# S5 split by token group, each half woven beside the other group's SwiGLU, two side steps for each main step

## The reference, cut to what matters

```python
x <- LN0(alpha*x + 0.5*SwiGLU_1(x))
x <- LN1(alpha*x + Mix_l(x))
x <- LN2(alpha*x + 0.5*SwiGLU_2(x))

def step(s, uc):                       # S5, 64 groups of 16 channels, 64 complex states per group
    bu = jnp.einsum('bcgh,gph->bcgp', uc.astype(jnp.complex64), b_bar)
    a_cum, s_loc = lax.associative_scan(_s5_combine, (a_elems, bu), axis=1)
    s_all = s_loc + a_cum * s[:, None]
    y = jnp.real(jnp.einsum('bcgp,ghp->bcgh', s_all, cm))
    return s_all[:, -1], y
...
g = jax.nn.gelu(y.astype(x.dtype))
return (g @ w_out) * jax.nn.sigmoid(g @ w_gate), s_re, s_im
```

## Time and profile before

| | us |
|---|---|
| device time, median of 3 runs | 2738.49 (2734.43 to 2738.73) |
| device time of the profiled execution | 2735.0 |
| span of its core in the profile | 2733.3 |
| mean granted TensorE clock | 0.939 of full speed |
| PE busy | 2436.1 (89%) |
| PEld busy | 2287.8 (84%) |
| DVE busy | 1707.0 (62%) |
| ACT busy | 998.7 (37%) |
| POOL busy | 496.3 (18%) |
| read from HBM | 370.35 MB, 138 GB/s over the span |

### The profile page before, as it was taken

How to read it: one execution, slowest core, us unless ns; L and a number is a source line. 1 busy time by engine, 2 the same in 40 slices (tenths; PEclk the granted TensorE clock), 3 DMA queues, 4 the chain that set the end, 5 groups by cost and what they waited for, 6 DMA issues and landing times. The chain is left out here.

```text
span 2733.3 us, 43046 instructions
## 1 busy us (share of the span) xinstructions
PE 2436.1 (89%) x17245; PEld 2287.8 (84%) x17245; DVE 1707.0 (62%) x2660; ACT 998.7 (37%) x1486; POOL 496.3 (18%) x559
## 2 busy tenths in 40 slices
PE   7999999989989999999999989994408799999996
PEld 7999989988876677988999989993306798999995
DVE  6666665666644556767555676555894467667554
ACT  3434443334432334424333344332203344434332
POOL 0711100033000122012100132005910022103003
PEclk9999999999999999989999999997557899999997
DMA  7665554344466865445555545541003555665452
GB/s 182 180 176 159 176 171 129 113 120 135 125 186 212 253 182 136 141 111 149 167 147 151 149 138 157 147 131 20 1 4 47 124 148 153 181 178 159 146 151 77
DMA packets 658616, 383.55 MB, mean 140 GB/s; under 512 B 29842, under 2 KB 629778, under 8 KB 658418
## 3 DMA queue, kind: packets, MB, share of 16 engines
q1 hardware_dynamic: 651890, 360.42, 46.6%
q0 software_dynamic: 6528, 20.37, 2.5%
HBM read 370.35 MB, written 6.19 MB: 138 GB/s over the span
## 5 line engine op out<-in xcount | busy, mean ns | idle before, releaser
L217 DVE TENSOR_TENSOR w_lo<-w_raw,w_hi 128x1024 fp32r<-128x1024 f32 (+1 forms) x648 | 801.5, 1240 | 593.8 <-ACT w_hi L208 592.2
L222 PE MATMUL ps<-x_hi,w_hi 128*128 128x256 f32 (+1 forms) x3200 | 962.4, 301 | 29.1 <-DVE w_lo L217 27.7
L223 PE MATMUL ps<-x_lo,w_hi 128*128 128x256 f32 (+1 forms) x3200 | 951.9, 297 | 0.0
L224 PE MATMUL ps<-x_hi,w_lo 128*128 128x256 f32 (+1 forms) x3200 | 951.3, 297 | 0.0
L208 ACT ACTIVATE w_hi<-w_raw 128x1024 fp32r<-128x1024 f32 (+1 forms) x648 | 668.8, 1034 | 623.1 <-PE ps L224 524.5
L222 PEld LDWEIGHTS ps<-x_hi,w_hi 128*128 128x128 f32 x3200 | 611.7, 191 | 42.8 <-DVE w_lo L217 30.8
L223 PEld LDWEIGHTS ps<-x_lo,w_hi 128*128 128x128 f32 x3200 | 612.1, 191 | 1.1 <-issue 0.2
L224 PEld LDWEIGHTS ps<-x_hi,w_lo 128*128 128x128 f32 x3200 | 611.6, 191 | 0.0
L222 PE MATMUL ps<-h_hi,w_hi 128*128 128x256 f32 (+1 forms) x1408 | 423.0, 300 | 11.7 <-DVE w_lo L217 10.7
L224 PE MATMUL ps<-h_hi,w_lo 128*128 128x256 f32 (+1 forms) x1408 | 417.4, 296 | 0.0
L223 PE MATMUL ps<-h_lo,w_hi 128*128 128x256 f32 (+1 forms) x1408 | 416.6, 296 | 0.0
(11 more groups left out here) (277 smaller groups left out, 2319.5 us busy)
## 6 DMA issues: line engine op xcount, KB each, us to landing
w_raw<-in_ffn_w_gate SPq DMA_DIRECT2D x176, 512.0 KB, 3.9
w_raw<-in_ffn_w_up SPq DMA_DIRECT2D x176, 512.0 KB, 3.9
w_raw<-in_ffn_w_down SPq DMA_DIRECT2D x128, 512.0 KB, 4.1
w_raw<-in_w_in_ab SPq DMA_DIRECT2D x56, 512.0 KB, 3.8
w_raw<-in_ffn_w_down SPq DMA_DIRECT2D x64, 384.0 KB, 3.4
arena<-in_cache_v POOLq DMA_DIRECT2D x64, 256.0 KB, 4.5
arena<-in_cache_k SPq DMA_DIRECT2D x64, 256.0 KB, 3.9
w_raw<-in_w_out_ab SPq DMA_DIRECT2D x16, 512.0 KB, 4.0
```

Of the source, the lines that this page charges most:

```text
L217: dve.tensor_tensor(T.w_lo[:, u % RING, 0:n], T.w_raw[:, u % RAW, 0:n], T.w_hi[:, u % RING, 0:n].bitcast(F32), ALU.subtract).then_inc(T.w_ ...
L222: pe.matmul(out, w_hi, m_hi, start=first, stop=False)
L223: pe.matmul(out, w_hi, m_lo, start=False, stop=False)
L224: return pe.matmul(out, w_lo, m_hi, start=False, stop=last)
```

## The change

Everything now lies in one block (`layers`). Four things move.

1. **Constants** (`S5Prepare`, 52 side steps): b_bar, the powers of B (now on POOL), the powers of C, their transposes and the taps are made beside the first SwiGLU (46 main steps of A and the first 16 of B) and stored in HBM, three tensors of 512 KB for each of 8 octets of groups.
2. **S5 by group** (`S5Group`, 11 input steps, 12 scan steps, 17 output steps, behind the norm's first 8): S5 of A is woven beside the SwiGLU of B that ends layer 0's work (`f1b`, 46 main steps), S5 of B beside the first two parts of A's last SwiGLU (`f3a[:2]`, 32 main steps). The three made tensors are loaded again for each group. `paced` lets two side steps of norm and S5 run for each main step (24 pairs).
3. **Norms and output products**: the norm of B before S5 is woven (it is the first part of the pairs); the output product of A is woven with a norm of B, that of B stands alone.
4. **Gate**: sigmoid becomes tanh, with the residual's factor doubled.

The core of the diff:

```diff
+def paced(steps, alone):
+
+    held = False
+    for i, _ in enumerate(steps):
+        held = not held and i not in alone
+        if not held:
+            yield
+    if held:
+        yield
...
+class S5Prepare:
...
+    FIRST, EVERY = 18, 4
+    STEPS = FIRST + EVERY * (KT - 1) + 6
+    TURN_C = 10
...
+    def load(self, q):
+        for r, part in enumerate(("re", "im")):
+            q.dma_start(self.b_raw[:, r], self.I["s5_b_" + part][0].rearrange("(a s) p h -> (s p) a h", s=2))\
+             .then_inc(self.S.b_loaded.h, 16)
...
+            q = self.at(i, 0)
+            if q is not None:
+                pe.wait_ge(S.formed.h, q + 1)
...
+            for lag, form, r in ((-8, form_b, 0), (-7, form_b, 1), (-6, form_c, 0), (-5, form_c, 1)):
+                q = self.at(i, lag)
+                if q is not None:
+                    form(q, r)
+            yield
...
+class S5Group:
+
+
+    INPUTS, SCAN = KT + 3, 12
+    OUTPUTS = 2 * KT + 1
+    STEPS = INPUTS + SCAN + OUTPUTS
...
+        def load(e):
+            n = self.octets + e
+            if n >= 2:
+                sp.wait_ge(S.mixed.h, n - 1)
+            sp.dma_start(self.taps[e % 2], S.made_taps[e].rearrange("p (i n) -> p i n", i=GT))\
+              .then_inc(S.spread[e % 2].h, 16)
+            sp.dma_start(self.decays[e % 2], S.made_decays[e].rearrange("p (i n) -> p i n", i=GT))\
+              .then_inc(S.spread[e % 2].h, 16)
...
+                for a in range(A4):
+                    for r in range(2):
+                        for s in range(2):
+                            mm = pe.matmul(T.ps[HALF[s], 7, (r * A4 + a) * c:(r * A4 + a + 1) * c],
+                                           self.b_rows[e % 2][:, r, a, HALF[s]], self.u[:, 2 * (A4 * e + a) + s, :],
+                                           start=True, stop=True)
+                mm.then_inc(S.added.h, 1)
...
+                for k in range(A4):
+                    for w in range(2):
+                        for s in range(2):
+                            j = s * A4 + k
+                            lhs, rhs = ((self.u[:, GT * e + j, :], self.taps[e % 2][:, j, :]),
+                                        (self.starts[e % 2][:, j, :], self.decays[e % 2][:, j, :]))[w]
+                            mm = pe.matmul(T.ps[s * HD:s * HD + c, 4 + s, k * P:(k + 1) * P], lhs, rhs,
+                                           start=(w == 0), stop=(w == 1))
+                mm.then_inc(S.mixed.h, 1)
...
+        wide = [P, GPAIRS, RUNS]
+        for j in range(1, RUN - 1):
+            advance([runs[:, r, :, :, j + 1] for r in range(2)], [runs[:, r, :, :, j] for r in range(2)], 0, wide)
+            yield
...
+        for a0 in (0, self.FIX):
+            self.fix(dve, T.dve_chain, self.part, a0)
+            yield
...
+            if i == self.INPUTS + 8:
+                pool.wait_ge(S.carried.h, self.n + 1)
+                for a0 in (2 * self.FIX, 3 * self.FIX):
+                    self.fix(pool, T.pool_chain, self.part_pool, a0)
...
+        def norm_and_s5(norm, s5):
+
+            return together(norm, after(idle(Norm.STEPS - 2), s5))
+
+        def beside_a(norm, s5):
+            return paced(norm_and_s5(norm, s5), ())
...
-            weave(ffn(ffn_tensor, pe, f0b[:1]), N0A.tensor(pe))
+            weave(after(ffn(ffn_tensor, pe, f0a), woven(ffn(ffn_tensor, pe, f0b[:1]), N0A.tensor(pe))),
+                  after(S5C.tensor(pe), after(load_tensor(T, pe, B, rows, turned[B]), prepare.tensor(pe))))
...
-            weave(ffn(ffn_tensor, pe, f2b), N3A.tensor(pe))
-            run(N3B.tensor(pe))
+            weave(ffn(ffn_tensor, pe, f2a[1:]), N1B.tensor(pe))
+            weave(ffn(ffn_tensor, pe, f1b), beside_a(N3A.tensor(pe), s5_a.tensor(pe)))
+            weave(out_tensor(T, pe, OA2), N2B.tensor(pe))
+            weave(ffn(ffn_tensor, pe, f2b), N4A.tensor(pe))
+            weave(ffn(ffn_tensor, pe, f3a[:2]), beside_b(N3B.tensor(pe), s5_b.tensor(pe)))
+            run(out_tensor(T, pe, OB2))
+            weave(ffn(ffn_tensor, pe, f3a[2:]), N4B.tensor(pe))
+            weave(ffn(ffn_tensor, pe, f3b), after(N5A.tensor(pe), store_columns(pe, A)))
+            run(after(N5B.tensor(pe), store_columns(pe, B)))
```

More of the change, by code:

```diff
@@ L94, in weave, with woven, together @@
         pass
+def woven(main, side):
+    for _ in main:
+        next(side, None)
+        yield
+    for _ in side:
+        yield
+def together(first, second):
+    going = True
+    while going:
+        going = False
+        for steps in (first, second):
+            for _ in steps:
+                going = True
+                break
+        if going:
+            yield
 def after(first, second):
@@ L1731, with open_s5 @@
     pass
[L1734 removed]
+def open_s5(ctx, T):
+    nc = T.nc
     S = S5()
@@ L1739, in sb, with count @@
         return ctx.enter_context(nc.sbuf_tensor("s5_" + name, shape, dt))
+    def count(name):
+        return Count(T.ctx, nc, "s5_" + name)
     S.powers = sb("powers", [P, 2, CL + 1, GPAIRS])
@@ L1744, in open_s5_constants @@
     S.skip = sb("skip", [GH, GROUPS])
-    return S
[L1748 to L1755, removed]
+    S.made_rows = nc.dram_tensor("s5_made_rows", (KT, P, 2 * A4 * P), F32, kind="Internal").ap()
+    S.made_decays = nc.dram_tensor("s5_made_decays", (KT, P, GT * P), F32, kind="Internal").ap()
@@ L2504, in first_layer @@
         f2b = parts(F2B, (0, 1, 2), N3B)
+        F3A = Ffn(A, ffn_3, N4A.ready, N4A.affine + KT)
+        f3a = parts(F3A, (0, 1))
+        s5_b = S5Group(T, M, S, B, N3B.affine + KT, (), s5_a)
+        N4B = Norm(T, B, 4, 2.0, True)
+        OB2 = Out(T, B, s5_w_out, s5_w_gate, N3B.affine + KT, N4B, ((S.rested, 2 * KT),))
+        N5A = Norm(T, A, 5, 2.0, False)
+        f3a += parts(F3A, (2,), N5A)
+        F3B = Ffn(B, ffn_3, N4B.ready, N4B.affine + KT)
+        N5B = Norm(T, B, 5, 2.0, False)
+        f3b = parts(F3B, (0, 1, 2), N5B)
+        before = {A: 0, B: 2 * len(A.tiles)}
+        whole = {A: N5A.affine + KT, B: N5B.affine + KT}
+        y_rows = cut(0, TT, D_MODEL)
         block = ctx.enter_context(nc.Block())
@@ L2517, in _ @@
             load_pieces(T, sp, RAW)
+            S5C.load(sp)
             for t in B.tiles[:-1]:
@@ L2615, in _ @@
             S5C.gpsimd(pool)
-            run(ffn(ffn_gpsimd, pool, f0a))
             pool.wait_ge(T.ln_loaded.h, 32)
-            weave(ffn(ffn_gpsimd, pool, f0b[:1]), N0A.gpsimd(pool))
+            weave(after(ffn(ffn_gpsimd, pool, f0a), woven(ffn(ffn_gpsimd, pool, f0b[:1]), N0A.gpsimd(pool))),
+                  after(idle(1 + KT), prepare.gpsimd(pool)))
             run(project_gpsimd(T, pool, PA, O))
```

1142 lines of the change are left out of this document (596 added, 546 removed).

## The result

| | before | after |
|---|---|---|
| device time, median of 4 runs each, same chip | 2736.64 (2734.43 to 2738.73) | 2715.51 (2711.96 to 2717.8) |
| ratio, 95% interval | | 0.9922 (0.9905 to 0.9939) |
| span of the profiled core | 2733.3 | 2714.4 |
| mean granted TensorE clock | 0.939 | 0.957 |
| PE, DVE, POOL busy | 2436.1, 1707.0, 496.3 | 2465.7, 1675.3, 599.0 |

What follows compares the result with a forecast made beforehand. PE was taken as the bound outside S5 and DVE inside it. 2429 + 132 + 51 + 20 + 25 + 11 + 8 = 2676 us of span, forecast as 2680 us device time, 2.1% faster, range 2608 to 2750.

Steps and rivals of the forecast that it cites:

- What bounds it, and what is removed: PE bounds the kernel outside S5, DVE inside; the 304 us stretch without weight products goes.
- no slice under 6 save around the scans: Sign expected in PE's row of the page after: low slices only around the two scans.
- PE's work, 132: PE's added small matmuls, transposes and taps in both S5 groups and the preparing: 132 us (111 to 170).
- halves overlap: Output matmuls alternating between halves of the array's columns: 2.4 us per octet taken instead of 3.6.
- Scan, 51, and clock, 8: PE waits for DVE's scan beside down steps, 51 us (35 to 85); lower clock behind two scans, 8 (3 to 30).
- Two steps at once, 20: Paired S5 steps: PE waits at each pair's second step and at output pairs, 20 us (5 to 40).
- Preparing beside the first SwiGLU, 25: First stage: waits for POOL's add at A's norm, slower w_lo and table loads, 25 us (5 to 65).
- Norms and outputs, 11: Woven norm N3B about 7 us, norm beside A's output product 4; together 11 (4 to 20).
- the base of 2429: Span of 2733.3 us less the 304 us stretch, before the added costs.
- POOL's bound: Rival: POOL bounds the first stage at 20.2 us an octet, 75 us of waits, total 2730; chance 0.13.
- loads that come late: Rival: three loads per octet delay weights on the same queue, 2 us in each of 16 pairs: 2715; chance 0.06.
- The lower clock: Rival, the slower case: woven stages run partly at 1.2 GHz, 47 us per tenth, 2773 at 20%; chance 0.11.

Runs made afterwards that it cites:

- e8: The changed kernel with an octet's 32 output matmuls ordered as 16 into one half of the array's columns, then 16 into the other: 2735.21 us.
- e6: The changed kernel without the recurrence's arithmetic (DVE's advances and POOL's fixes left out, steps, waits and copies kept): 2654.78 us.
- e5: The changed kernel with a main step for each of the scan's 12 steps, all other steps still two at a time: 2657.22 us.
- e1: The changed kernel with a third buffer for the powers of C instead of two: 2688.34 us.
- e3: The changed kernel with only octet 0 of the prepared tensors stored and every S5 load reading octet 0: 2686.65 us.
- e11: The changed kernel with a third buffer for the powers of C and one of three wide POOL instructions kept per half-form: 2663.89 us.

## Why the prediction was right, and where it was wrong

- **What bounds it, and what is removed.** Right: PE's hole of 304 us is gone, and PE is at nine tenths nearly everywhere. But "no slice under 6 save around the scans" failed: slice 4 is at 5.
- **PE's work, 132.** Right, at some 136. Per group: outputs 21.9 us (19 forecast, bounds 14 and 29), increments 9.0 (8), turning gelu back 9.0 (10), chunk transposes 8.4 (8.8), second transposes 5.4 (4), from PE's rows between 1475 and 1799 us. Preparing 17.1 for taps and 9.3 for transposes, 26 (30). The guess that halves overlap was worth 13.4 us of PE's time a group in e8.
- **Scan, 51, and clock, 8.** Right in size: 61 by e6, against 59. DVE was busy 44.1 of 50 us from 1550 and 46.3 from 2160, near the 45 forecast. The wait stood mostly at the outputs' first matmul, not at w_lo. What I failed to see is how much of the price was one of placement: with a main step for each scan step its waits fell from 49 to 19 us (e5).
- **Two steps at once, 20.** Right for the output pairs: 14.5 us at L2223 (12.8 forecast), only beside up steps. The input pairs cost 2.2 us (at L2152) where 7 stood.
- **Preparing beside the first SwiGLU, 25.** This is the term that was mis-sized. The stage costs 102.5 where 55 stood, with 59 us of waits where 25 stood. The step that failed is that POOL "reaches the add it needs after 6.5 octets, at 233: PE waits 8 to 10": it took POOL as an engine that never waits. POOL waited 67.4 us for stores, the add came at 292.10, and PE waited 20.5 us for it. The prediction followed the three loads of an octet in the S5 stages, but not the 13 stores here, four of which free POOL's buffer and are queued on SP behind weight loads. The loop is worth 29 us by e1. The second part that failed is POOL's rate at the norm's adds, 25 us more with its slowing of w_lo, where I had 20 for both. The third is a term that was put at nothing: the clock of this stage, 0.93 and 0.97, some 17 us.
- **Its range for that term, 5 to 65,** holds the 59 us of waits, but not the 76 (102.5 - 26) that the preparing cost beyond its matmuls.
- **Norms and outputs, 11.** No run touches this term. As all terms but the first stage's came out 9 below in sum, and the measured ones above came out no lower than forecast in sum, either it or the base of 2429 was put too high; which, stays open. That the span erred by 38 us and not by the first stage's 47.5 is luck.
- **The rivals.** POOL's bound was real: that rival put 75 us of waits into the first stage, and 59 were measured, the loop among them. In the first stage loads that come late fell with e3; for the three loads an octet beside S5, which that rival meant, no run changes them, but with the scan out PE waits only 5.8 us for w_lo there. The lower clock did come in a part of a stage: 0.91 from 120 to 293 us and 0.90 from 293 to 380, beside 0.63 to 0.90 around the scans. In whole stages it stayed at 0.93 or more, so the slower case did not come. By that rival's own figure, 47 us a tenth, the gain of 58 is gone from 12% on, not from 15%.
- **Open.** The 48 us left in e11, without the loop and with a third of POOL's products, are some 26 of PE's matmuls, 15 of waits (38.7 us of PE idle against 23.6 in before: 8.6 more at w_lo, 6.2 at gate) and 6 of busy time that goes with a clock of 0.97 to A's mark. What of these waits is the third of POOL's work that stayed, and what the tables' loads, no run parted.

## What to carry to other kernels

When work moves to another place of in-order streams, list each buffer that it reuses, and ask on which queue the operation stands that frees it and what stands ahead of it. A store that is issued behind waiting loads ties an engine that never seemed critical to the slowest one. And count cover step by step, not over a stage: a POOL step of 5 us beside main steps of 2.8 is late even when the totals agree, and a scan that made 49 us of waits with two steps to a main step made 19 with one.

## What the runs showed of the hardware

- SP's issue of one of these stores took 0.60 us (taps) and 0.63 (decays) in the median of after, against 0.37 for a weight load. With all but octet 0's left out, the time was 2 us below the third buffer's, within the spread.
- Two fp32 matmuls into different halves of the array's columns (and different PSUM banks) overlapped to 0.62 of their time end to end (21.9 against 35.3 us for 256), and for the kernel 20 us hung on the order of a loop.
- The granted clock of after was 0.75 in a stretch with PE busy 10.65 of 25 us and 0.63 in one with 5.66 of 25. It was at 0.89 and 0.90 in the 100 us behind the first, with PE busy 44 and 45 of 50; with the scan's steps alone and PE full from 1650 to 1700 us it was 1.00.
- In the stage where POOL's lateness kept PE waiting, the clock was 0.93 and 0.97, against 1.00 in the same stage of before.
